# Row statistics spread over turned inputs in place of transposes, and a convolution that alternates between two chunks

## What is computed

```python
def rmsnorm(x, g):
    y = xf * lax.rsqrt(jnp.mean(xf * xf, axis=-1, keepdims=True) + EPS)
    return y * g

def mixer(x, ...):
    h = rmsnorm(x, g_mix)
    z = h @ w_in                      # 1024 -> 2048
    x_rnn, g_rnn, glu_a, glu_b = jnp.split(z, ...)     # 512 channels each
    xr = depthwise_conv(x_rnn, conv4_w, conv4_b, ...)
    y_rnn = rg_lru_bidir(xr, ...) * gelu(g_rnn)
    c = glu_a * sigmoid(glu_b)
    c = depthwise_conv(c, conv31_w, conv31_b, (15, 15))      # 31 taps
    c = silu(layernorm(c, conv_ln_g, conv_ln_b))
    return concatenate([rmsnorm(y_rnn), rmsnorm(c)]) @ w_out

x = x + mixer(x)
x = x + mem_cross_attn(x, mem)        # uses rmsnorm(mem, g_mem)
x = x + peer(x)                       # 128 gathered experts per token
return rmsnorm(x, g_final)
```

## Time and profile before

| | us |
|---|---|
| median of 3 runs | 4158.22 (4154.7 to 4163.09) |
| the profiled execution, its own time | 4158.18 |
| its span in the trace | 4156.4 |
| PE busy | 3723.5 (90%) |
| DVE busy | 2651.4 (64%) |
| ACT busy | 1708.5 (41%) |
| POOL busy | 1739.4 (42%) |
| 120 convolution steps on DVE (L906), busy | 200.9 |
| 1280 gathers (L502), busy on POOL | 1603.2 |

### The profile page before, as it was taken

How to read it: one execution, slowest core, us unless ns; L and a number is a source line. 1 busy time by engine, 2 the same in 40 slices (tenths; PEclk the granted TensorE clock), 3 DMA queues, 4 the chain that set the end, 5 groups by cost and what they waited for, 6 DMA issues and landing times.

```text
span 4156.4 us, 34979 instructions
## 1 busy us (share of the span) xinstructions
PE 3723.5 (90%) x8916; PEld 1625.8 (39%) x8916; DVE 2651.4 (64%) x5680; ACT 1708.5 (41%) x4553; POOL 1739.4 (42%) x1485
## 2 busy tenths in 40 slices
PE   8999979979789989988988998988998998998877
PEld 4554444434334434433433433433433433443322
DVE  2346972266685785686686586587587577578544
ACT  4343223024344444445444444444444444444333
POOL 0001232034345444444444445444444444455665
PEclk9999999989999999999999999999999999999999
DMA  3002546189999999999999999999999999999998
GB/s 108 31 31 94 190 172 238 51 341 404 418 417 421 421 420 406 418 421 403 420 421 405 417 421 407 415 421 403 418 421 413 415 421 402 422 421 419 410 422 356
DMA packets 210650, 1462.58 MB, mean 352 GB/s; under 512 B 25616, under 2 KB 25744, under 8 KB 41872
## 3 DMA queue, kind: packets, MB, share of 16 engines
q0 software_dynamic: 194880, 1377.92, 80.7%
q1 hardware_dynamic: 15568, 82.43, 5.5%
HBM read 1424.61 MB, written 35.65 MB: 351 GB/s over the span
## 4 chain that ended last, share of the span: by engine, by line
PE 34%; DMA 25%; DVE 15%; issue 6%; POOL 5%; ACT 5%; ACTq 1%; DVEq 1%; POOLq 0%; PEldq 0%
DMA arena<-in_uv,arena 24%; PE ps L1392 19%; PE ps L1412 10%; DVE arena L950 5%; DVE arena L906 5%; POOL arena L502 5%; PE ps L1376 3%; ACT arena L671 1%; ACT L667 1%; ACT gated L669 1%; PE ps L1404 1%; ACT acts L667 1%; PE ps L1310 1%; ACTq L668 0%; DVE arena L1021 0%
## 5 line engine op out<-in xcount | busy, mean ns | idle before, releaser
L1392 PE MATMUL ps<-arena 128*128 128x512 f32 x5120 | 2393.7, 613 | 362.0 <-ACT arena L671 359.1
L502 POOL DMA_INDIRECT arena<-in_uv,arena x1280 | 1603.2, 1252 | 1656.6 <-PE ps L1392 1115.3
L950 DVE SCALAR_TENSOR_TENSOR arena<-arena 128x1024 f32<-128x1024 f32 x1280 | 1552.5, 1223 | 955.3 <-DMA arena<-in_uv,arena 947.0
L1392 PEld LDWEIGHTS ps<-arena 128*128 128x128 f32 x5120 | 954.8, 193 | 1746.5 <-issue 966.8
L667 ACT ACTIVATE acts<-dots 128x1 f32<-128x1 f32 x1280 | 258.0, 202 | 1694.2 <-DVE arena L950 1680.0
L1412 PE MATMUL ps<-arena 128*128 128x512 f32 x1280 | 574.4, 592 | 0.0
L671 ACT ACTIVATE arena<-ident,gated 128x128 f32<-128x128 f32 x1280 | 514.1, 402 | 93.1 <-issue 6.6
L1412 PEld LDWEIGHTS ps<-arena 128*128 128x128 f32 x1280 | 243.4, 190 | 306.3 <-issue 306.3
L1274 PE MATMUL ps<-arena 128*128 128x512 f32 (+1 forms) x768 | 278.6, 522 | 3.5 <-DVE arena L794 2.9
L669 ACT ACTIVATE gated<-arena,acts 128x1 f32<-128x1 f32 x640 | 188.5, 294 | 45.9 <-issue 2.4
L669 ACT ACTIVATE gated<-GAT,acts 128x1 f32<-128x1 f32 x640 | 188.5, 295 | 45.1 <-issue 1.4
(11 more groups left out here) (185 smaller groups left out, 1999.0 us busy)
## 6 DMA issues: line engine op xcount, KB each, us to landing
arena<-in_items SPq DMA_DIRECT2D x32, 1024.0 KB, 5.6
arena<-in_uv,arena POOLq DMA_INDIRECT x1280
qk_scratch<-arena POOLq DMA_DIRECT2D x32, 256.0 KB, 2.6
wp_scratch<-arena POOLq DMA_DIRECT2D x32, 256.0 KB, 6.0
vo_scratch<-arena POOLq DMA_DIRECT2D x32, 256.0 KB, 2.6
arena<-qk_scratch SPq DMA_DIRECT2D x2, 4096.0 KB, 14.4
arena<-vo_scratch SPq DMA_DIRECT2D x2, 4096.0 KB, 21.7
arena<-wp_scratch SPq DMA_DIRECT2D x2, 4096.0 KB, 27.5
```

The lines of the kernel that those rows point to most:

```text
L502: g.indirect_dma_start(out=ring[r], out_offset=None, in_=a["uv"], in_offset=bass.IndirectOffsetOnAxis(ap=IDXC[:, k:k + 1], axis=0))\
L950: v.scalar_tensor_tensor(out=ring[r][:, 0:D], in0=ring[r][:, 0:D], scalar=1.0, in1=H[par], op0=ALU.mult, op1=ALU.mult, accum_out=dots[:, r ...
L1392: ins = t.matmul(ACC[par][:, half * BANK:(half + 1) * BANK], diag[r], ring[r][:, D + half * BANK:D + (half + 1) * BANK], start=False, stop ...
```

## The change

Two inputs are added: `xt`, the tokens turned (128 channels x 8 groups x 1280 tokens), and `memt`, the memories turned (128 x 8 x 512). They are loaded straight into `hT` and `mT`, in three batches of tokens (512, 512, 256) and one of memories. The blocks as rows still come in, for their sums of squares. ACT squares the blocks of a batch and takes one root for the batch; DVE inverts it; ACT writes for each block a diagonal matrix of the inverted roots (128x128) into the slot; PE multiplies the matrix of ones by it (`spread_rstd`, L1289), which puts the factor of each token on all partitions of bank 6 or 7; DVE multiplies `hT` in place by the channel's gain and this row (`scale_turned`, L833), eight instructions a batch. The convolution takes two chunks by turns, so that each step waits for the step before the previous one, and `SUM_CONV` becomes (42, 68, 70).

```diff
@@ -80,7 +80,7 @@
 AT_CENTER, AT_TANH, AT_SILU = (75, 76, 77, 78), (92, 93, 94, 95), (96, 98, 100, 102)
 
 
-SUM_CONV, SUM_VAR, SUM_SQUARES = (42, 60, 69), (77, 78, 79), (100, 102, 104)
+SUM_CONV, SUM_VAR, SUM_SQUARES = (42, 68, 70), (77, 78, 79), (100, 102, 104)
...
+BATCHES = [(0, 4), (4, 8), (8, NB), (NB, NB + MB)]
+TOKEN_BATCHES = 3
...
-        def turned(i):
-
-            return bank(4 if i < NB and i % 2 == 0 else 6, 2)
+        def spread(m):
+
+            return bank(6 + m % 2)
...
             def load_x(i):
                 if i >= XSLOTS:
-                    sp.wait_ge(tr_done, i - XSLOTS + 1)
+                    sp.wait_ge(spread_done, 1 + (i - XSLOTS) // 4)
...
+            def load_turned(m):
+                lo, hi = BATCHES[m]
+                if m < TOKEN_BATCHES:
+                    dst, src = hT[:, :, lo * P:hi * P], a["xt"][:, :, lo * P:hi * P]
+                else:
+                    dst, src = mT, a["memt"]
+                sp.dma_start(dst, src).then_inc(xt_load[m], 16)
+
             for i in range(4):
                 load_x(i)
+            load_turned(0)
             load_item(0)
-            for i in range(4, XSLOTS):
+            for i in range(4, 8):
                 load_x(i)
+            load_turned(1)
+            load_x(8)
+            load_x(9)
+            load_turned(2)
             sp.wait_ge(gm_zero, 1)
             for e in range(2):
                 sp.dma_start(gm[64 * e:64 * e + 64, :, 64 * e:64 * e + 64], a["gates"][e])\
                   .then_inc(s_gm, 16)
             load_item(1)
-            for i in range(XSLOTS, NB + MB):
+            for i in range(NB, NB + MB):
                 load_x(i)
+            load_turned(TOKEN_BATCHES)
             for j in range(2, Z_ITEMS + 2):
...
             act.wait_ge(eps_ready, 1)
-            for i in range(NB + MB):
-                act.wait_ge(s_xload[i % XSLOTS], 16 * (i // XSLOTS + 1))
-                if i >= 1:
-                    act.wait_ge(rstd_ready, i)
-                link(act.activation(AF[:, 0:D], x_slots[i % XSLOTS], ACT.Square, accum_out=ms))
-                act.activation(rs, ms, ACT.Sqrt, scale=1.0 / D, bias=eps).then_inc(std_ready, 1)
-                act.wait_ge(rstd_ready, i + 1)
-                act.activation(x_slots[i % XSLOTS], x_slots[i % XSLOTS], ACT.Copy, scale=rs).then_inc(xn_ready, 1)
+            act.wait_ge(ident_ready, 3)
+
+            def token_squares(m):
+                for i in range(*BATCHES[m]):
+                    act.wait_ge(s_xload[i % XSLOTS], 16 * (i // XSLOTS + 1))
+                    ins = act.activation(x_slots[i % XSLOTS], x_slots[i % XSLOTS], ACT.Square, accum_out=rr[:, i:i + 1])
+                link(ins)
+                each = rr[:, BATCHES[m][0]:BATCHES[m][1]]
+                act.activation(each, each, ACT.Sqrt, scale=1.0 / (D * (CH * P) ** 2), bias=eps_ones)\
+                   .then_inc(std_ready, 1)
+
+            def token_diagonals(m):
+                act.wait_ge(rstd_ready, m + 1)
+                for i in range(*BATCHES[m]):
+                    ins = act.activation(x_slots[i % XSLOTS][:, 0:P], ident[:, :], ACT.Copy, scale=rr[:, i:i + 1])
+                ins.then_inc(xn_ready, 1)
+
+            token_squares(0)
+            for m in range(len(BATCHES) - 1):
+                if m == 0:
+                    token_diagonals(0)
+                    token_squares(1)
+                else:
+                    token_squares(m + 1)
+                    token_diagonals(m)
+            token_diagonals(len(BATCHES) - 1)
             act.wait_ge(s_cols, 16)
...
 
-            v.memset(eps, EPS).then_inc(eps_ready, 1)
-
-            def recip_rstd(i):
-                v.wait_ge(std_ready, i + 1)
-                v.reciprocal(rs, rs).then_inc(rstd_ready, 1)
-
-            def evacuate(i):
-
-                v.wait_ge(tr_done, i + 1)
-                dst = hT[:, :, i * P:(i + 1) * P] if i < NB else mT[:, :, (i - NB) * P:(i - NB + 1) * P]
-                g = col("g_mix" if i < NB else "g_mem", 0, KD)
-                v.tensor_tensor(dst, turned(i).rearrange("p (k t) -> p k t", k=KD),
-                                g.unsqueeze(2).to_broadcast([P, KD, P]), ALU.mult).then_inc(ht_ready, 1)
+            v.memset(eps, EPS)
+            v.memset(eps_ones, EPS / (CH * P) ** 2).then_inc(eps_ready, 1)
+
+            def token_rstd(m):
+                v.wait_ge(std_ready, m + 1)
+                each = rr[:, BATCHES[m][0]:BATCHES[m][1]]
+                v.reciprocal(each, each).then_inc(rstd_ready, 1)
+
+            def scale_turned(m):
+
+                v.wait_ge(xt_load[m], 16)
+                v.wait_ge(spread_done, m + 1)
+                lo, hi = BATCHES[m]
+                for k in range(KD):
+                    part = hT[:, k, lo * P:hi * P] if m < TOKEN_BATCHES else mT[:, k, :]
+                    ins = v.scalar_tensor_tensor(part, part, col("g_mix" if m < TOKEN_BATCHES else "g_mem", k),
+                                                 spread(m)[:, 0:(hi - lo) * P], ALU.mult, ALU.mult)
+                ins.then_inc(ht_ready, 1)
 
             v.wait_ge(s_cols, 16)
-
-            behind = {i: i + (1 if i < 5 else 2 if i < 9 else 3) for i in range(NB)}
-            for i in range(NB + MB):
-                recip_rstd(i)
-                for j in range(NB):
-                    if behind[j] == i:
-                        evacuate(j)
+            for m in range(TOKEN_BATCHES):
+                token_rstd(m)
+                if m:
+                    scale_turned(m - 1)
+            scale_turned(TOKEN_BATCHES - 1)
+            token_rstd(TOKEN_BATCHES)
 
 
...
             v.tensor_tensor(sp4, acc, z2, ALU.add).then_inc(const_half, 1)
-            for i in range(NB, NB + MB):
-                evacuate(i)
+            scale_turned(TOKEN_BATCHES)
...
-            for c in range(CH):
-                w = [col("conv31_w", j * CH + c) for j in range(TAPS31)]
-                link(v.tensor_scalar(xp(c, 0, L31), ci(c, 0, L31), w[0], col("conv31_b", c), ALU.mult, ALU.add))
-                for j in range(1, TAPS31):
-                    ins = v.scalar_tensor_tensor(xp(c, 0, L31), ci(c, j, L31), w[j], xp(c, 0, L31),
-                                                 ALU.mult, ALU.add)
-                    if j < TAPS31 - 1:
-                        link(ins)
-                ins.then_inc(conv_ready, 1)
+            for pair in ((0, 1), (2, 3)):
+                seen = {}
+                for j in range(TAPS31):
+                    for c in pair:
+                        w = col("conv31_w", j * CH + c)
+                        if j:
+                            v.wait_ge(dve_own, seen[c])
+                            ins = v.scalar_tensor_tensor(xp(c, 0, L31), ci(c, j, L31), w, xp(c, 0, L31),
+                                                         ALU.mult, ALU.add)
+                        else:
+                            ins = v.tensor_scalar(xp(c, 0, L31), ci(c, 0, L31), w, col("conv31_b", c),
+                                                  ALU.mult, ALU.add)
+                        if j == TAPS31 - 1:
+                            ins.then_inc(conv_ready, 1)
+                            continue
+                        own[0] += 1
+                        ins.then_inc(dve_own, 1)
+                        seen[c] = own[0]
             v.wait_ge(mean_done, 1)
...
-            def turn_block(i):
-
-                t.wait_ge(xn_ready, i + 1)
-                if i >= 2:
-                    t.wait_ge(ht_ready, i - 1 if i < NB else i)
-                for k in range(KD):
-                    ins = t.transpose(turned(i)[:, k * P:(k + 1) * P], x_slots[i % XSLOTS][:, k * P:(k + 1) * P],
-                                      ident[:, :])
-                ins.then_inc(tr_done, 1)
+            def spread_rstd(m):
+
+                t.wait_ge(xn_ready, m + 1)
+                if m >= 2:
+                    t.wait_ge(ht_ready, m - 1)
+                lo, hi = BATCHES[m]
+                for i in range(lo, hi):
+                    ins = t.matmul(spread(m)[:, (i - lo) * P:(i - lo + 1) * P], ones512[:, :],
+                                   x_slots[i % XSLOTS][:, 0:P], start=True, stop=True)
+                ins.then_inc(spread_done, 1)
 
 
...
-            zs, blocks = 0, 0
+            zs = 0
+            spread_rstd(0)
             for n, job in enumerate(JOBS):
-                if 0 < n <= MB:
-                    turn_block(NB + n - 1)
+                if n == 1:
+                    spread_rstd(TOKEN_BATCHES)
                 if n >= 2:
                     prev = n - 2
                     if taker(JOBS[prev]) == "act":
@@ -1265,11 +1314,10 @@
                     w = item(zs // 2)[:, (zs % 2) * D:(zs % 2 + 1) * D]
                     for lo, size in tiles(T):
                         if n == 0:
-                            need = (lo + size) // P
-                            while blocks < min(need + 1, NB):
-                                turn_block(blocks)
```

(19 more changed lines are left out.)

## The result

The changed kernel takes 4204.66 us (median of 4 runs, 4202.92 to 4207.15), the kernel before in the same session 4157.77 (4154.7 to 4163.09): a ratio of 1.0112, interval 1.0094 to 1.0129. It is 47 us slower, where 10 us faster was forecast. The profiled execution took 4207.15 us, its span is 4205.4.

The account below looks back on a forecast made before the run. PE was taken to bound the first 700 us, with DVE almost level, and the last stage to wait for gathered rows. + 5.7 - 3.1 - 11.8 - 1.1 = -10.3 us from 4158.18 gave 4147.9 us, range 4142 to 4157.

Parts of the forecast that it names:

- The failed step: Convolution: POOL's second sum stands behind a store, takes 2.49 us with DVE idle and ends at 561.5.
- It is the one place ahead of the last stage where DVE's convolution holds PE up: At the mean behind job 72: PE idles 12.09 us for POOL's sum of the four convolved chunks.
- an overlap that doesn't come about: Rival 1, convolution: DVE does not overlap its steps, pace stays 1.60 us, total 4163.3 us; chance 0.11.
- The steps overlap: DVE's convolution: steps start 1.42 us apart in place of 1.60, so 120 steps save 21.6 us.
- rival 2: Convolution: the overlap is partial, pace 1.51 us, 3 us of stall remain, about 4151 us; chance 0.13.
- PE's stall at the mean goes: Ahead of the mean products: 11.8 of 12.09 us of stall go; the products take 3.61 us, 1.1 less.
- The front: Start to job 4: 5.7 us lost up to job 1, 3.1 us back behind it, net 2.6 us later.
- rival 3: Front loads: turned tokens in 2 KB pieces load slowly; at 204 GB/s the total is 4160.8 us; chance 0.07.
- What is won ahead of the last stage reaches the end: Last stage: none of its instructions is edited, so time won ahead moves its start and reaches the end unshortened.
- the convolution's gain: Convolution and mean: 11.8 us of stall and 1.1 us of faster mean products, together 12.9 us.

Follow-up runs that it names:

- e5: Kernel before's front, with the changed convolution by turns and every fourth step waiting for the step just before: 4148.01 us, ratio 0.9977 to the kernel before.
- e1: The changed front alone, with the convolution, its waits and SUM_CONV of the kernel before: 4166.82 us, ratio 1.0015 to the kernel before.
- e3: The changed kernel, but each convolution step waits for the one right before it, so nothing overlaps: 4168.59 us, ratio 1.0018 to the kernel before.
- e4: The changed kernel, but every fourth convolution step waits for the step just before it: 4155.44 us, ratio 0.9987 to the kernel before.
- e12: e9 with one more waiting step, at the 13th tap of the third chunk: 4150.66 us, ratio 0.9983 to the kernel before, one group.
- e6: e4 with ACT's diagonals of batch 2 called ahead of the squares of the memory blocks: 4149.59 us, ratio 0.998 to the kernel before.
- e8: e7 with a wait for the step just before at every twelfth step in place of every fourth: 4140.94 us, ratio 0.9958 to the kernel before.
- e7: e4 with ACT's squares and diagonals batch by batch, DVE scaling each batch right behind its inversion: 4143.71 us, ratio 0.9961 to the kernel before.
- e9: The changed kernel with the wait at every fourth step in chunks 0 and 1 only: two groups, 4146.6 to 4151.2 and 4203.6 to 4211.1 us.

## Why the prediction was wrong

**The failed step** is in the convolution's part: "POOL. It sends the store ... and its second sum now stands there: 2.49 us with DVE idle". I priced POOL's sums by their rows of before, 2.49 and 2.90 us, and asked only whether the work ahead of them was done. That they could run at all while DVE never pauses I took for granted. The costliest sums are not in my working at all: the three over the squares of `y_rnn`, whose result PE needs while the first pair runs, stood at nothing, and they are where 46 us went. I worked out what a faster DVE brings forward and what it makes late, and not what DVE's small gaps were good for. The sentence that went with it, "It is the one place ahead of the last stage where DVE's convolution holds PE up", was true of before and false of the change. I also had two rows the wrong way round: the sum of 2.49 us at 531.11 ran while DVE convolved, and the one of 2.90 us at 575.15 behind DVE's last step. None of my rivals had POOL shut in; the only one on the slow side of the convolution was an overlap that doesn't come about, and it was the overlap that did come about which shut POOL in: 45.75 us of waiting for PE at the first pair, 5.36 at the second.

The rows were there. Before, the first sum of POOL and the convolution step beside it:

```profile
376.05 3.67 POOL L429 TENSOR_TENSOR arena<-arena 128x1282 f32<-128x1282 f32 x1 [371.74 <-ACT arena L589]
376.99 4.09 DVE L906 SCALAR_TENSOR_TENSOR arena<-arena,cols 128x1295 f32<-128x1295 f32 x1
```

The sum is 1.2 us longer than the 2.49 of the earlier trace rows, and the step of 1.57 us lasts 4.09. Read together: POOL calls at 376.05 in the middle of a step, gets in when that ends at 376.95, and holds the next step until 379.7. So the two exclude each other, and POOL gets in between two steps. Whoever sees that must ask what happens when there is no between. (Which of the two came first the recorded starts don't always tell: at 531.11 the sum took its 2.49 us although a step had stood in the trace since 530.74, and it was that step which lasted 4.24.)

The Trainium skill, SBUF — State Buffer, section "Who interferes with whom", has the pair: a VectorE instruction with two inputs in SBUF contends with a GpSimd instruction that reads SBUF, for a shared port that is an exclusive lock. I had not weighed it. The trace agrees that the two exclude each other (4.09 us against 1.57). By the same page of the Trainium skill, section "Summary: rules for kernel authors", the second to issue is blocked "until the first finishes". As an estimate from that and the rows, a sum called in the middle of a step would start at most 1.57 us late and last some 4 us; the runs show 83.58. That overlapping steps hand the port on among themselves is my reading; no run tells it from another cause in DVE or POOL, and overlapping steps with one SBUF input were not tried. POOL's stores, which only issue transfers, took their usual 0.72 us beside such steps.

**Point by point.**

- *The steps overlap*: right in kind. The pace is 1.48 us, where I took 1.42 from a pair with a constant and rival 2 put 1.51. The Trainium skill, VectorE: DVE Perf Modes, section "The DRAIN you can't avoid", says that leaving out the semaphores saves nothing, and allows that an instruction that is not held starts earlier. The first would leave the pace at 1.60; the trace disagrees, with 1.48 against a duration of 1.57. The whole convolution takes 373.51 to 562.24, 188.7 us, against 366.38 to 575.08, 208.7: 20.0 us saved of 21.6 forecast. 120 x 0.12 = 14.4 us of it is pace; most of the other 5.6 is that POOL's sums hold DVE up less often.
- *PE's stall at the mean goes*: right, 12.09 us to 0.43, and the mean products take 2.44 us where I put 3.61. But by then PE came 62 us later, so this row proves little; e5 does, with 1.30 us of stall left and 10.2 us won.
- *The front*: mis-sized. Forecast +5.7 at job 1, measured 60.40 - 50.77 = +9.6; forecast -3.1 behind it, measured 112.97 - 60.40 = 52.6 for three jobs against 55.2, -2.6. Net +7.1 in place of +2.6, and e1 gives +6.8 at the end. Two terms failed. I let the last memory block land at 42.0 with one square behind it. There was one square behind it, at 44.83, but the block landed at 44.81 (the four at 40.99, 42.27, 43.54 and 44.81, each with its square right behind): tile 1 started at 47.49 in place of 45.3. Of these 2.8 us, 0.8 lie in the start of my sum (before, the last block landed at 30.03 and not at 29.2), and 0.9 in the first four blocks, there at 9.86 where it had been 8.94; the rest is in the turned batches (next point). And tiles 1 and 2 took 12.18 us in place of 10.6: PE had idled 3.4 us ahead of them and was at a granted clock of 0.50 to 0.66 behind it. That does not happen in every execution: those profiled for e3, e4 and e12 idled 2.7 to 3.0 us there and took 10.49, as e6 does without the wait. The stretches (us, PE busy, clock, DMA share, GB/s):

```profile
12.00:14.00 2.00, 0.00 (x0) 1.00 1.09 412
...
26.00:28.00 2.00, 0.00 (x0) 1.00 1.05 407
...
32.00:34.00 2.00, 0.45 (x2) 1.00 1.31 198
...
48.00:50.00 2.00, 2.00 (x4) 0.50 0.12 49
50.00:52.00 2.00, 2.00 (x4) 0.66 0.00 0
```

I had charged a fallen clock to tile 0 and not to these.
- *The turned loads are slow* (rival 3): a little. The two batches with rows of 2 KB landed 5.37 and 5.41 us behind the load before them (at 15.23 and 28.20), some 390 GB/s each where I took 410 (412 and 407 in the first two stretches above, which lie inside them). The third has 256 tokens, so its rows are of 1 KB and not of 2, as I had written for all: 1.05 MB in 3.72 us, 282 GB/s, with the gates' pieces of 256 bytes in the queue right behind it (198 GB/s in 32 to 34 us).
- *What is won ahead of the last stage reaches the end*: right in sign, with losses too. +50.1 us at `mix_out` were +49.0 in the span.

In short, of the terms of the sum the front was short by 4.5 us, the convolution's gain was four fifths of its size (10.2 of 12.9, in e5), and a term of some +55 us was missing: the two waits for POOL with the clock behind them.

## What to carry to other kernels

A wait is not only a loss: a chain that waits on itself leaves gaps, and another engine may live in them. Before removing them, look for instructions of the two engines that lengthen each other in the trace (a step of 1.57 us that lasts 4.09 beside a sum), and for who needs the other engine's result while the chain runs; of the 20.0 us by which the convolution got shorter, one kept wait in four steps left 13.8 (e4) and one in twelve 16.6 (e8), without the 46 us of waiting. And where one stage's statistics of all blocks stand behind loads, call them block group by block group, in the order in which they are needed: that made a front that lost 7 us (e1) into one that wins 4 over the front of before (e7's 4143.71 against e5's 4148.01, same session).

## What the runs showed of the hardware that I had not expected

- A POOL sum over SBUF that lasts 2.5 us alone lasted 83.6 us beside an unbroken row of DVE steps of two SBUF inputs that overlap by 0.09 us, and a gap of 0.03 us let such a sum in (e12). Having called ahead of 54 of the steps gave POOL no turn. But up to three boundaries behind a gap it got in where the steps overlap.
- It also got in where DVE changed to `tensor_scalar` (L950, one input in SBUF): at 463.93 two of these took 6.96 us in place of 1.82, with POOL's sums beside them. Whether the change of kind or the boundary itself opens the way no run tells apart.
- Once in, POOL got in again and again: in e8 three overlapping steps in a row lasted 4.1 to 4.2 us, the third beside a sum that was called 0.5 us after the one before it had ended.
- The same program fell into two times some 60 us apart (e9); that a call of POOL near the last opening decides it is inferred.
